# Pairs of feed-forward steps by a seven-product scheme: from three spread pairs in three stages to four adjacent pairs in four stages

## The reference

```python
x = x + 0.5 * swiglu(rms_norm(x, g), w_gu, w_down)      # ffn0 to ffn3
x = x + (silu(h2 @ w_gate) * (h2 @ w_up)) @ w_down      # ffn4
```

## Time and profile before

| | |
|---|---|
| median of three runs | 1307.35 us |
| the profiled execution | 1312.76 us |
| its span on the core | 1311.0 us |
| PE busy | 1293.4 us, 99% of the span |
| DVE busy | 893.2 us, 68% |
| ACT busy | 774.8 us, 59% |
| moved by DMA | 256.40 MB, 196 GB/s in the mean |

### The profile page before, as it was taken

The page is one execution under the profiler, slowest core; times in us unless marked ns, Lnnn a source line. Parts: engine busy times, 40 slices in busy tenths (PEclk is TensorE's granted clock), DMA queues, the critical chain, the costliest instruction groups (busy, mean ns, idle before and its releaser), DMA issues.

```text
span 1311.0 us, 17106 instructions
## 1 busy us (share of the span) xinstructions
PE 1293.4 (99%) x7012; PEld 1083.9 (83%) x7012; DVE 893.2 (68%) x1062; ACT 774.8 (59%) x1019; POOL 31.2 (2%) x49
## 2 busy tenths in 40 slices
PE   7999999999999999999999999999999999999998
PEld 6888888888988888888787888888888898888887
DVE  5554446868457877866353566678778699688785
ACT  6544438756557665665543467576556767665654
POOL 0000000000000000000000000000000000000000
PEclk9999999999899999999999999999999999999999
DMA  8545544332039789365444533398892533688761
GB/s 321 204 179 191 185 170 184 138 129 98 34 116 354 242 266 332 99 272 193 144 176 161 176 103 126 107 366 271 270 319 92 218 138 129 248 265 316 232 222 33
DMA packets 38894, 256.40 MB, mean 196 GB/s; under 512 B 4316, under 2 KB 6620, under 8 KB 8992
## 3 DMA queue, kind: packets, MB, share of 16 engines
q1 hardware_dynamic: 31488, 208.86, 43.2%
q0 software_dynamic: 6192, 43.79, 12.3%
q10 hardware_dynamic: 1136, 2.66, 0.6%
HBM read 254.23 MB, written 2.11 MB: 196 GB/s over the span
## 4 chain that ended last, share of the span: by engine, by line
PE 95%; ACT 2%; DVE 2%; issue 1%; DMA 1%; SPq 0%; ACTq 0%; DVEq 0%
PE ps L2432 25%; PE ps L2434 24%; PE ps L2433 24%; PE ps L2347 8%; PE ps L2358 1%; PE ps L2465 1%; PE ps L2473 1%; PE ps L2478 1%; PE ps L2583 1%; PE ps L2488 1%; PE ps L481 1%; PE ps L483 1%; PE ps L482 1%; ACT w_hi_part L579 1%; PE ps L2523 1%
## 5 line engine op out<-in xcount | busy, mean ns | idle before, releaser
L1473 DVE TENSOR_TENSOR w_lo_part<-w_raw,w_hi_part 128x2048 fp32r<-128x2048 f32 (+2 forms) x172 | 389.1, 2265 | 198.4 <-ACT w_hi_part L579 197.4
L579 ACT ACTIVATE w_hi_part<-w_raw 128x2048 fp32r<-128x2048 f32 (+2 forms) x171 | 324.2, 1897 | 195.3 <-PE ps L2434 179.2
L2432 PE MATMUL ps<-w_hi_part,x_hi 128*128 128x512 f32 (+1 forms) x860 | 335.9, 391 | 0.8 <-DVE w_lo_part L1473 0.5
L2434 PE MATMUL ps<-w_hi_part,x_lo 128*128 128x512 f32 (+1 forms) x860 | 328.9, 382 | 0.0
L2433 PE MATMUL ps<-w_lo_part,x_hi 128*128 128x512 f32 (+1 forms) x860 | 328.0, 381 | 0.0
L2434 PEld LDWEIGHTS ps<-w_hi_part,x_lo 128*128 128x128 f32 x860 | 161.6, 188 | 32.3
L2432 PEld LDWEIGHTS ps<-w_hi_part,x_hi 128*128 128x128 f32 x860 | 161.8, 188 | 31.3 <-ACT arena L709 1.1
L2432 PE MATMUL ps<-w_hi_part,h_hi_part 128*128 128x512 f32 x464 | 186.7, 402 | 0.0
L2433 PEld LDWEIGHTS ps<-w_lo_part,x_hi 128*128 128x128 f32 x860 | 162.0, 188 | 29.0
L2434 PE MATMUL ps<-w_hi_part,h_lo_part 128*128 128x512 f32 x464 | 181.4, 391 | 0.0
L2433 PE MATMUL ps<-w_lo_part,h_hi_part 128*128 128x512 f32 x464 | 180.9, 390 | 0.0
(11 more groups left out here) (433 smaller groups left out, 1491.1 us busy)
## 6 DMA issues: line engine op xcount, KB each, us to landing
w_raw<-in_tiles SPq DMA_DIRECT2D x167, 1024.0 KB, 4.9
arena<-in_tiles SPq DMA_DIRECT2D x27, 1024.0 KB, 6.8
t<-in_tiles POOLq DMA_DIRECT2D x18, 1024.0 KB, 10.2
arena<-in_tiles POOLq DMA_DIRECT2D x18, 1024.0 KB, 9.3
w_raw<-in_tiles SPq DMA_DIRECT2D x3, 512.0 KB, 7.1
arena<-in_w_ukv POOLq DMA_DIRECT2D x1, 1536.0 KB, 13.1
arena<-in_w_dkv POOLq DMA_DIRECT2D x1, 1280.0 KB, 7.4
w_raw<-in_tiles SPq DMA_DIRECT2D x2, 536.0 KB, 3.7
```

What stands on the lines that cost most here:

```text
L579: nc.scalar.activation(WH[:, n % RING, 0:w], source(n), ACT.Copy).then_inc(S["w_hi"], 1)
L1473: nc.vector.tensor_tensor(WL[:, n % RING, 0:w], source(n), WH[:, n % RING, 0:w], ALU.subtract).then_inc(S["w_split"], 1)
L2432: nc.tensor.matmul(o, a_hi, w_hi, start=start, stop=False, skip_group_check=True)
L2434: return nc.tensor.matmul(o, a_lo, w_hi, start=False, stop=stop, skip_group_check=True)
```

## The change

The stage ffn0 becomes paired as well, and each of the four paired stages has four pairs, at steps 3, 5, 7 and 9, directly one after the other; only steps 0, 1 and 2 stay plain. Step 10 is now taken ahead of step 9 at the end (`TURN_ORDER`).

In a pair the products are p5, m2, m1, p3, m6, m7, m4 in this order, with down steps around m7. p3 goes onto p5 in the same bank, and the snapshots change accordingly. The raw tiles of m1, m2 and p3 travel in SP's ring; the `PB` buffers and their loads are gone. T1 stands in one of two buffers `TA`; DVE adds p3's raw tile to it, in place, for T2 (one sum of 128 by 2048 instead of two), and a third adding transfer of POOL makes T4 from it. T3 has a buffer `TC` of its own.

In ffn0 the memory is loaded into `T8` in two transfers, its squares (`mem_squares`) are taken right after `w_hi` of g0(1), and its turning is spread over the pairs. In all paired stages the norm (`first`) is moved ahead of `w_hi` of g0(1). The order of ACT, DVE and PE in `paired_ffn` is rewritten. The bias rows (line 3626) are issued after all sums of ffn3.

```diff
-PAIRED = ("ffn1", "ffn3", "ffn4")
-PAIR_STEPS = (3, 6, 9)
+PAIRED = ("ffn0", "ffn1", "ffn3", "ffn4")
+PAIR_STEPS = (3, 5, 7, 9)
+TURN_ORDER = [0, 1, 2, 3, 4, 5, 6, 7, 8, 10, 9]
...
+    order = [("g0", 0), ("g1", 0), ("g0", 1), ("g1", 1), ("d", 0), ("g0", 2), ("g1", 2)]
+    for s in PAIR_STEPS:
+        order += [("p5", s), ("m2", s), ("m1", s), ("p3", s), ("m6", s), ("d", s - 2), ("m7", s), ("d", s - 1), ("m4", s)]
+    return order + [("d", 10), ("d", 9)]
...
                 if r >= RING:
-                    sp.wait_ge(S["w_split"], ring[r - RING][0] + 1)
+                    before_it = ring[r - RING][0]
+                    sp.wait_ge(S["w_split"], before_it + 1)
+                    if kind_of.get(before_it, ("", "", 0))[1] == "p3":
+                        sp.wait_ge(S["sums"], sum_no[kind_of[before_it][0], "t2", kind_of[before_it][2]])
...
-                for u in range(4):
-                    turned_hi(name, u)
+                if name != "ffn0":
+                    for u in range(4):
+                        turned_hi(name, u)
+                first()
                 w_hi(at("g0", 1))
+                if more:
+                    more(0)
                 w_hi(at("g1", 1))
-                first()
...
                 def t2(s):
-                    q_ready(s, 2)
-                    dve.wait_ge(S["w_split"], at("m1", s) + 1)
-                    dve.wait_ge(S["t_added"], 32 * pair_no(name, s) + 16)
-                    nc.vector.tensor_tensor(PB[0], T8F, PB[2], ALU.add).then_inc(S["sums"], 1)
-
-                def t4(s):
-                    q_ready(s, 3)
-                    dve.wait_ge(S["w_split"], at("m2", s) + 1)
-                    dve.wait_ge(S["sums"], sum_no[name, "t2", s])
-                    nc.vector.tensor_tensor(PB[3], PB[0], PB[3], ALU.add).then_inc(S["sums"], 1)
+                    r = ring_no[at("p3", s)]
+                    dve.wait_ge(S["w_split"], at("p5", s) + 1)
+                    dve.wait_ge(w_loaded[r % RING], 16 * (r // RING + 1))
+                    a = pair_source(name, "m6", s)
+                    nc.vector.tensor_tensor(a, a, RAW[:, r % RING, :], ALU.add).then_inc(S["sums"], 1)
```

DVE's order for one inner pair (ACT's is alike), as it stands after the change:

```diff
+                w_lo(at("m4", 5))
+                w_lo(at("p5", 7))
+                t2(7)
+                w_lo(at("m2", 7))
+                hidden(5, 1, bank(4)[:, CW:], SG[:, 1, :])
+                hidden(6, 1, P5F[:, CW:], P5F[:, 0:CW])
+                w_lo(at("m1", 7))
+                hidden_lo(5)
+                w_lo(at("p3", 7))
+                w_lo(at("m6", 7))
+                c11(7)
+                w_lo(at("d", 5))
+                hidden_lo(6)
+                c12(7)
+                w_lo(at("m7", 7))
+                w_lo(at("d", 6))
+                hidden(7, 0, C11F[:, CW:], C11F[:, 0:CW])
+                hidden(8, 0, C12F[:, CW:], C12F[:, 0:CW])
+                c22(7)
```

PE's pair:

```diff
                 def pair_of_steps(s):
...
+                    s_product("p5", s, 7, True, False)
+                    turn_pair(s - 1 if s == PAIR_STEPS[0] else s - 2)
+                    x_product("m2", s, 5, 0, 1, True, True)
+                    if s > PAIR_STEPS[0]:
+                        turn_pair(s - 1)
                     x_product("m1", s, 4, 0, 0, True, False)
                     pe.wait_ge(S["snap"], 3 * pair_no(name, s) + 1)
+                    s_product("p3", s, 7, False, True)
+                    pe.wait_ge(S["sums"], sum_no[name, "c11", s])
                     s_product("m6", s, 4, False, False)
+                    down_half(s - 2, 0)
+                    down_half(s - 2, 1)
+                    pe.wait_ge(S["sums"], sum_no[name, "c12", s])
                     s_product("m7", s, 4, False, False)
...
+                    down_half(s - 1, 0)
+                    down_half(s - 1, 1)
...
+                    pe.wait_ge(S["sums"], sum_no[name, "c22", s])
                     x_product("m4", s, 4, 1, 1, False, True)
```

POOL's queue:

```diff
+            def t4_sum(name, s):
+                split(name, "m6", s)
+                pool.dma_start(pair_source(name, "m4", s), stored(name, "g1", s), accum_op=ALU.add).then_inc(S["t4_added"], 16)
...
+                t1_base(name, 3)
+                t1_sum(name, 3)
+                split(name, "g0", 1)
+                t3_base(name, 3)
+                t3_sum(name, 3)
+                split(name, "g0", 2)
+                pool.wait_ge(S["norm_sd"], norm_no[name] + 1)
+                t1_base(name, 5)
+                t4_sum(name, 3)
+                t1_sum(name, 5)
+
+            def later_sums(name):
+
+                for s in PAIR_STEPS[1:]:
+                    split(name, "m7", s - 2)
+                    t3_base(name, s)
+                    if s < PAIR_STEPS[-1]:
+                        split(name, "m4", s - 2)
+                        t1_base(name, s + 2)
+                    t3_sum(name, s)
+                    if s < PAIR_STEPS[-1]:
+                        t1_sum(name, s + 2)
+                    t4_sum(name, s)
```

More of the change, by code:

```diff
@@ new lines, in paired_ffn @@
+                if more:
+                    more(2)
+                gate_of(P5F, 5, "c22", 1)
+                w_hi(at("m2", 7))
+                gate_21(5)
+                w_hi(at("m1", 7))
+                hidden_hi(5)
+                w_hi(at("p3", 7))
+                w_hi(at("m6", 7))
+                snap(P5F, 7, "p5", 7)
+                snap(C11F, 5, "m2", 7)
+                w_hi(at("d", 5))
+                hidden_hi(6)
+                w_hi(at("m7", 7))
+                gate_of(C11F, 7, "c11", 0)
@@ L786, in paired_ffn @@
+                snap(C12F, 7, "p3", 7)
+                w_hi(at("d", 6))
+                gate_of(C12F, 7, "c12", 0)
+                w_hi(at("m4", 7))
+                w_hi(at("p5", 9))
+                if more:
+                    more(3)
+                gate_of(P5F, 7, "c22", 1)
+                w_hi(at("m2", 9))
+                gate_21(7)
                 w_hi(at("m1", 9))
-                hidden_hi(6)
-                gate(8, 0)
-                gate(8, 1)
                 hidden_hi(7)
-                w_hi(at("m2", 9))
+                w_hi(at("p3", 9))
@@ L1538, in ffn, with paired_ffn @@
                         early(s)
-            def paired_ffn(f, name, start, first):
+            def paired_ffn(f, name, start, first, more=None):
                 def at(kind, s):
@@ new lines, in paired_ffn @@
+                w_lo(at("m1", 5))
+                hidden_lo(3)
+                w_lo(at("p3", 5))
+                w_lo(at("m6", 5))
+                c11(5)
+                w_lo(at("d", 3))
+                w_lo(at("m7", 5))
+                c12(5)
+                w_lo(at("d", 4))
+                hidden_lo(4)
+                hidden(5, 0, C11F[:, CW:], C11F[:, 0:CW])
+                hidden(6, 0, C12F[:, CW:], C12F[:, 0:CW])
+                c22(5)
+                w_lo(at("m4", 5))
+                w_lo(at("p5", 7))
@@ new lines, in later_sums @@
+            def later_sums(name):
[9 more added lines that the diff above has]
+                    t4_sum(name, s)
+            for name in ("ffn0", "ffn1"):
+                first_sums(name)
+                later_sums(name)
```

503 lines of the change are left out of this document (204 added, 299 removed).

## The result

The changed kernel takes 1351.37 us (median of 4 runs, 1347.7 to 1354.47), the one before in the same comparison 1308.42 (1307.13 to 1312.12): a ratio of 1.0324 [1.0301, 1.0347], 42.9 us slower. The forecast was 1319.5 us with a range up to 1334. The sign and the place were right, the size was not. The profiled execution took 1350.4 us with a span of 1348.2, against 1312.76 and 1311.0: 37.2 us of span to explain.

The account below looks back on a forecast made before the run. PE bounds the kernel, but full DMA engines were to stall it in the new pairs: -16.8 (products saved) + 26 (stalls) + 3 (start) = +12.2 us, put on the median 1307.35: 1319.5 us, range 1296 to 1334.

Parts of the forecast that it names:

- PE's saving: Paired stages: seven more pairs, each saving 2.40 us of products on PE, -16.8 us.
- The pair's length without waits: Paired stages: seven products, two down steps and two turns take 31.0 us on PE.
- DVE and ACT at no cost: Pairs: DVE carries 28.2 us, ACT 22, in 31.0 of PE; each tile arrives in time, 0 us.
- Rival (c): Pairs: DVE's fixed order at 91% decides, not DMA; every pair loses 1 us, 1309.5 us; chance 0.1.
- The price of an adding transfer: DMA engines: an adding tile costs two plain ones, 5.3 us against 2.6.
- Rival (b): DMA engines: an adding transfer costs what a plain one does, 2.6 us; no stall, 1293.5 us; chance 0.07.
- The stalls: Four paired stages: full DMA engines make tiles late for PE, 6.5 us per stage between 0 and 10, +26 us.
- The walk: Paired stages, order followed: from m6(3)'s split to m4(7), 78.3 us of transfers against 73.5 of PE, 4.8 late.
- Rival (a): Paired stages: slack covers the DMA overload, 0 to 2 us of stall per stage, 1294 to 1302 us; chance 0.2.
- The start: First stage: reordered ACT work delays g0(1) by 1.2 us and g1(1) by 1.6, +3 us, bounds 0 and 6.
- Marks: Signs of being right: DMA share 0.97 and over, some 320 GB/s from p5(3) to m4(7); ACT's ffn1 DMA waits above 6.1 us.
- From the profiled execution to the median: Whole kernel: the profiled execution, 1312.76 us, lay 5.4 us above the runs' median, 1307.35; the forecast was put on the median.

Follow-up runs that it names:

- fourth buffer: Changed kernel with a fourth raw buffer for d(s-2) of each pair, asked for behind p3's load: 1320.51 us, ratio 1.0093.
- no adding transfer: Changed kernel with all three adding transfers of a pair made plain, same bytes, queues, waits and order: 1299.18 us, ratio 0.9928.
- after: The changed kernel itself, measured beside the kernel before: 1351.37 us, ratio 1.0324.
- the probe: Kernel before, with 4, 5, 6 and 7 extra ACT copies at four steps of plain ffn0 to stall PE: 1335.37 us, ratio 1.0204.
- the version with the fourth buffer and the second one for T3: Changed kernel with the fourth raw buffer for d(s-2) and, in ffn1, ffn3 and ffn4, a second T3 buffer: 1335.10 us, ratio 1.0199.

## Why the prediction was right and wrong

- **PE's saving (-16.8): right.** PE's busy time falls by 16.4 us where no stretch at 0.50 is (fourth buffer), and the rest in the account from 1305.9 to between 1286 and 1293. The pair's length without waits was forecast as 31.0 us and is 31.28.
- **DVE and ACT at no cost: right.** 176.00 us of 176 busy with no adding transfer. Rival (c) is out.
- **The price of an adding transfer (twice a plain one, 5.3): right in kind, a little high.** 4.8 to 5.0 by the pair's length with full engines. (The pair with its plain step took 48.1 us before, from p5(6) at 485.5 to p5(9) at 533.6, and not 46.9; no term of the sum uses it.) Rival (b) is out: it would make after and the version without adding equal, and they are 52 us apart. The fit that the Trainium skill gives (DMA: Bandwidth & Descriptors, Anatomy of one DMA) makes no difference for adding transfers; the trace does not agree, with 4.8 against 2.6 us.
- **The stalls (+26, 6.5 a stage between 0 and 10): the step that failed in the stages,** measured 35.4, 8.9 a stage. The walk took the channel as full from the split of m6(3) to m4(7) and made T1(5), then T2's and T4's tiles the late ones. With the fourth buffer something like that happens and costs 16.6 us, 4.1 a stage. In after the largest share, 22 us of gaps, comes from a tile that the walk never listed: d(s-2), which can be asked for only once a place in the ring is free and then needs 12 us. Nor is the channel full: from 492 to 507 in ffn1 its share is 0.74, as SP asks for no tile between 493.3 and 507.8, and GpSimd's queue, waiting for a split, for none between 490.8 and 501.2. The sum of transfers was counted, the moment from which each may be asked for was not, except for T1, T2 and T4. T1(5) late was foreseen, and where it shows too (ahead of m2(5)): some 2 us a stage were forecast, and the gaps around p5(5) are 3.3.
- **The clock (no term): the step that was missing.** 41.0 us of the span were granted 0.50 against 10.2 before, worth +10.6 to +15.4. The forecast priced a gap by its length. Over its +12.2 us of span the measured +37.2 has 9.4 more of stalls, up to 15.4 of clock, 1.7 of start, and 1.5 less of PE. The clock alone doesn't explain the miss of the range: without it the result would be 1336 to 1341, still over 1334.
- **Rival (a), no more than 2 us of stall a stage, is out** with 8.9. Its mark, landings of adding transfers near 10 us, doesn't tell: their medians in after are 8.9 (T3), 10.8 (T4) and 13.4 us (T1), beside these stalls.
- **The start (+3, bounds 0 and 6): 4.7,** one gap ahead of g0(1) and none at g1(1), where 1.6 was forecast; from 25.1 to 31.9 us the granted clock was 0.50. What undoing it gives back is not settled: 1.3 us in after, with 16 us of scatter.
- **Marks.** A share of 0.97 and over at 320 GB/s throughout holds for the fourth buffer (1.01 to 1.04, 277 to 346), in after only in parts. ACT's waits on the ring's tiles in ffn1: 10.0 us, and 9.9 on GpSimd's, against 6.1. From the first turn of pair 3 to that of pair 9 the stages ffn1, ffn3 and ffn4 are 14.6, 12.4 and 14.6 us longer than without adding transfers, alike as forecast.
- **From the profiled execution to the median** I took 5.4 us off; after's own profiled execution lay 1.0 us under its median. That is about 6 of the 32 us by which the forecast missed.

What stays open: what makes a gap bring the low clock. In after gaps of 2.7 and 3.0 us were followed by it and one of 3.5 in ffn0 was not; in the probe 2.49 and 3.96 us were not, nor was the start's gap of 2.9 with the fourth buffer. In the version with the fourth buffer and the second one for T3, two gaps of 1.8 us, 2.2 us from start to start, were. So the length of a gap alone doesn't decide. Whether the channel is relieved by making T4(7) or T3 in another way than by an adding transfer wasn't tried.

## What to carry to other kernels

Count DMA work in engine time, not bytes, and give an adding transfer about two plain ones. Then write beside each load the earliest moment at which it may be asked for and the latest at which it may land: a channel near full turns a tile with a late first moment into a stall, and asking earlier for a tile helps only if no sooner wanted one stands behind it. Where PE was gapless, price a new gap at more than its length, because the clock behind it may halve.

## What the runs showed of the hardware

- An adding transfer of 1024 KB costs the sixteen engines an estimated 4.8 to 5.0 us (pairs with full engines), a plain one 2.6; landing rises with it, 8.4/10.8/12.9 us against 5.0/6.7/8.6 for the same requests made plain.
- At or behind gaps of 2.3 to 8.3 us PE's granted clock was often 0.50, for 3.4, 6.8 or 10.2 us, in which large matmuls stand 0.43 us apart instead of 0.23; it was 1.00 behind the gaps of up to 2.1 us in the pairs with the fourth buffer.
- Plain ring loads that stand beside adding transfers take up to 16.5 us from issue to landing in after (median 5.8 over the kernel), 20.1 with the fourth buffer, against 13.9 before.
